# Conditioning matrix behind the first embedding summed on VectorE; first key slot computed one token tile at a time

## What is computed

```python
def per_layer_embed(h, p_i, g, w_gate, w_proj):
    gate = jax.nn.sigmoid((rms_norm(h, g) @ w_gate))
    return h + gate * (p_i @ w_proj)

# layer 1 of the first block
kvp = rms_norm(h, kv_norm) @ w_kv             # keys and values, 2048 columns
q = rms_norm(h, norm_mix[1]) @ b_w_q          # queries, 1024 columns
o = stick_breaking_attention(q, k, v)
h = h + o @ b_w_o

# second block
cond = jax.nn.silu(c)                         # 1 x 1024
mod = cond @ w_ada + b_ada                    # 1024 x 6144, 24 MB of weights
shift_m, scale_m, gate_m, shift_f, scale_f, gate_f = jnp.split(mod, 6, axis=-1)
h = modulate(rms_norm_2(x, g_pre_mix), shift_m, scale_m)
```

## Time and profile before

| | us |
|---|---|
| Median of 3 executions | 2948.27 |
| Lowest and highest of them | 2947.35, 2952.21 |
| The profiled execution | 2960.54 |
| Its span, first to last instruction | 2958.7 |
| PE busy | 2623.4 (89%) |
| DVE busy | 1368.7 (46%) |
| ACT busy | 616.2 (21%) |
| POOL busy | 489.4 (17%) |

### The profile page before, as it was taken

How to read it: one execution, slowest core, us unless ns; L and a number is a source line. 1 busy time by engine, 2 the same in 40 slices (tenths; PEclk the granted TensorE clock), 3 DMA queues, 4 the chain that set the end, 5 groups by cost and what they waited for, 6 DMA issues and landing times.

```text
span 2958.7 us, 28660 instructions
## 1 busy us (share of the span) xinstructions
PE 2623.4 (89%) x9706; PEld 1223.0 (41%) x9706; DVE 1368.7 (46%) x3391; ACT 616.2 (21%) x1232; POOL 489.4 (17%) x526
## 2 busy tenths in 40 slices
PE   8998787887799998787888799889999999999998
PEld 7663333333366663333333366543333232333333
DVE  5657777776425656777776541431111111111111
ACT  3022212232115122222232120211111111111111
POOL 0124333333200124333333200000000000000000
PEclk9999999999999999999999999889999999999999
DMA  5699999999863699999999833447999999899997
GB/s 217 264 377 422 421 421 421 421 420 421 347 240 143 249 377 422 421 421 421 421 421 421 345 127 114 180 199 321 422 422 422 422 422 422 352 422 422 376 400 295
DMA packets 145293, 1049.90 MB, mean 355 GB/s; under 512 B 16272, under 2 KB 16528, under 8 KB 17968
## 3 DMA queue, kind: packets, MB, share of 16 engines
q0 software_dynamic: 74064, 537.56, 43.8%
q1 hardware_dynamic: 70560, 509.12, 42.2%
q10 hardware_dynamic: 576, 2.13, 0.2%
HBM read 1047.69 MB, written 1.05 MB: 354 GB/s over the span
## 4 chain that ended last, share of the span: by engine, by line
PE 54%; DMA 37%; DVE 4%; ACT 2%; issue 1%; another core or an unknown queue 1%; DVEq 1%; SPq 0%; POOLq 0%
PE psum L566 14%; DMA big<-in_moe 13%; DMA uv_more<-in_peer_uv,rows_of 13%; DMA big<-in_peer_uv,rows_of 11%; PE psum L971 11%; PE psum L463 7%; PE psum L997 5%; PE psum L478 5%; PE psum L883 1%; PE psum L952 1%; PE psum L665 1%; PE psum L582 1%; DVE big L1598 1%; DVE uv_more L1598 1%; PE psum L965 1%
## 5 line engine op out<-in xcount | busy, mean ns | idle before, releaser
L566 PE MATMUL psum<-big,gdiag 128*128 128x512 f32 x1880 | 912.7, 642 | 233.1 <-ACT gdiag L1080 233.1
L1598 DVE CUSTOM_DVE_ANT_0 big<-psum,big 128x1024 f32<-128x1024 f32 x470 | 574.4, 1224 | 281.4 <-DMA big<-in_peer_uv,rows_of 274.8
L566 PEld LDWEIGHTS psum<-big,gdiag 128*128 128x128 f32 x1880 | 375.6, 205 | 761.9 <-issue 440.8
L2010 POOL DMA_INDIRECT big<-in_peer_uv,rows_of x470 | 444.7, 946 | 1158.2 <-PE psum L566 779.5
L971 PE MATMUL psum<-big 128*64 128x512 f32 x2240 | 500.9, 596 | 24.4 <-POOLq L2032 23.9
L1976 DVE TENSOR_SCALAR big<-psum 128x512 f32<-128x512 f32 x35 | 24.2, 692 | 667.5 <-PE psum L971 667.5
L971 PEld LDWEIGHTS psum<-big 128*64 128x64 f32 x2240 | 152.8, 137 | 370.7 <-issue 275.1
L997 PE MATMUL psum<-ring,big 128*64 128x512 f32 x1120 | 248.1, 594 | 3.8
L463 PE MATMUL psum<-big,ring 128*128 128x256 f32 x1088 | 241.2, 381 | 0.8 <-DVE big L1362 0.8
L463 PEld LDWEIGHTS psum<-big,ring 128*128 128x128 f32 x1088 | 206.5, 191 | 33.2 <-issue 3.8
L1074 ACT ACTIVATE gelu<-dots,rstd 128x4 f32<-128x4 f32 x128 | 38.0, 297 | 869.1 <-DVE dots L1598 869.1
(11 more groups left out here) (385 smaller groups left out, 1969.2 us busy)
## 6 DMA issues: line engine op xcount, KB each, us to landing
big<-in_moe SPq DMA_DIRECT2D x256, 1024.0 KB, 20.7
ring<-in_moe SPq DMA_DIRECT2D x128, 1024.0 KB, 19.4
big<-in_ada SPq DMA_DIRECT2D x24, 1024.0 KB, 11.8
ring<-in_peer_wq SPq DMA_DIRECT2D x16, 1024.0 KB
ring<-in_mix_in SPq DMA_DIRECT2D x14, 1024.0 KB
ring<-in_a_in SPq DMA_DIRECT2D x8, 1024.0 KB
ring<-in_ple_gate SPq DMA_DIRECT2D x8, 1024.0 KB
ring<-in_kv SPq DMA_DIRECT2D x8, 1024.0 KB
```

Source lines behind the costliest of these rows:

```text
L566: mm = pe.matmul(psum[:, OUT_BANK[t] + c, :], gdiag[:, n % DIAGS, :], uv[(PICKS * l + n) % ROWS][:, D + c * 512:D + (c + 1) * 512], start= ...
L1598: j = dve.tensor_tensor_reduce(out=u, in0=x, in1=u, scale=1.0, scalar=0.0, op0=ALU.mult, op1=ALU.add, accum_out=dots[:, n:n + 1])
L2010: pool.indirect_dma_start(uv[g % ROWS], None, table, bass.IndirectOffsetOnAxis(rows_of[:, n:n + 1], 0)).then_inc(uv_loaded[g % ROWS], 16)
```

## The change

Slots 4 to 7 of the conditioning are now summed on DVE by `sums`, as the others are: after `gains` of tile 1, four in a row. `condition_aside`, `take_aside` and `mod_rows` are gone; PE's four `turn_condition` stand after the second `qkv` slot. The turn of tile 0 (`turn(3, first, (0,), 6)`) stands between the two gate tiles, and DVE applies its two gains in `ple` (`first_gains`). The first `qkv` slot is done by `features_by_tile`, with the turn of tile 1 inside. `side` for part 1 lies elsewhere, since `qbT` and `xT2` now overlap its time.

```diff
             (4096, 6144, 2048, 8192, 10240, 12288, 14336, 16384),
-            (6144, 8192, 10240, 14336, 16384, 18432, 24576, 30720),
+            (8192, 10240, 14336, 16384, 18432, 22528, 24576, 30720),
...
             def turn_condition(s):
 
-                if 4 <= s < 8:
-                    pe.wait_ge(cond_took, s - 3)
-                    x = mod_rows[:, s % 2, :]
-                else:
-                    pe.wait_ge(sums_ready, s % 4 + s // 8 * 4 + 1)
-                    x = side[s // 4][s % 4 * 2][:, 0, :]
+                pe.wait_ge(sums_ready, s + 1)
+                x = side[s // 4][s % 4 * 2][:, 0, :]
...
                     mm.then_inc(tile_done, 1)
-                    if l and s == 0:
-                        turn(6, first, (0,), 6)
-                if l:
-                    return
-                pe.wait_ge(cond_ready, 1)
-                spare = ENDS[FIRST["ple_gate0"] + 1] % 3
-                condition_aside(4, 6)
-                condition_aside(5, 7)
-                turn_condition(4)
-                condition_aside(6, spare)
-                turn_condition(5)
-                pe.wait_ge(prod_taken, 2)
-
-            def last_condition():
-                turn_condition(6)
-                condition_aside(7, ENDS[FIRST["ple_gate0"] + 1] % 3)
-                turn_condition(7)
+                    if s == 0:
+                        turn(3 * l + 3, first, (0,), 6)
+
+            def features_by_tile(stage, i, known):
+
+                n = FIRST[stage]
+                w = slot_in(n).rearrange("p (k f) -> p k f", k=KC)
+                m = ENDS[n] - 2
+                for t in range(TT):
+                    if t:
+                        turn(i, hs, (1,))
+                    pe.wait_ge(xT_ready, known[t])
+                    for g in range(2):
+                        if t == 0:
+                            bank_free(m + g)
+                        for f in range(2):
+                            c = (2 * g + f) * P
+                            for k in range(KC):
+                                mm = pe.matmul(psum[:, (m + g) % 3, f * T + t * P:f * T + (t + 1) * P], w[:, k, c:c + P],
+                                               xT[:, k, t * P:(t + 1) * P], start=(k == 0), stop=(k == KC - 1))
+                        if t:
+                            mm.then_inc(tile_done, 1)
...
-            turn(3, first, (0,))
-            turn(3, hs, (1,))
-            last_condition()
-            pe.wait_ge(xT_ready, 20)
...
-            features("qkv", 0, xT)
+            features_by_tile("qkv", 3, (14, 20))
             features("qkv", 1, xT2)
+            for s in range(4, 8):
+                turn_condition(s)
+            pe.wait_ge(prod_taken, 2)
             pe.wait_ge(late_loaded, 16)
...
-                if l == 0:
-                    take_aside(4, 6)
-                    take_aside(5, 7)
                 root(7 + 7 * l, 1)
...
+            def first_gains(out, gain):
+
+                for b in range(2):
+                    dve.wait_ge(turned, 12 + b + 1)
+                    x = psum[:, 6 + b, :].rearrange("p (a b) -> p a b", a=4)
+                    k = slice(4 * b, 4 * b + 4)
+                    dve.tensor_tensor(out[:, k, 0:P], x, wide(gain[:, k], P), ALU.mult).then_inc(xT_ready, 1)
...
                 if l:
                     gains(6, gm, shift=shift_m, tiles=(0,), banks=6)
+                else:
+                    first_gains(xT, V8("kv_norm"))
                 dve.wait_ge(prod_done, 2 * l + 2)
...
                 j.then_inc(prod_taken, 1)
                 dve.drain()
+                if l == 0:
+                    first_gains(xT2, V8("norm_mix1"))
                 dve.tensor_tensor(h[:, 1, :], h[:, 1, :], ple_t[:, 1, :], ALU.add)
...
-            gains(3, V8("kv_norm"), gain2=V8("norm_mix1"))
+            gains(3, V8("kv_norm"), gain2=V8("norm_mix1"), tiles=(1,))
+            for s in range(4, 8):
+                sums(s)
             modulation(1)
```

More of the change, by code:

```diff
@@ L217, in build @@
             (4096, 6144, 2048, 8192, 10240, 12288, 14336, 16384),
[1 row of a table removed]
[1 row of a table added]
             (2048, 4096, 8192, 10240, 12288, 14336, 16384, 18432))]
         unit = sb("unit", [P, 1])
-        mod_rows = sb("mod_rows", [P, 2, 512])
         shift_m, scale_m, gate_m, shift_f, scale_f, gate_f = (modv[:, 8 * i:8 * i + 8] for i in range(6))
@@ L347, in build @@
         side_loaded = [sem(f"side_loaded{i}") for i in range(4)]
-        cond_took, aside_done = sem("cond_took"), sem("aside_done")
         rows_known, lru_exp, ro_taken = sem("rows_known"), sem("lru_exp"), sem("rec_out_taken")
@@ L506, in spread @@
                 mm.then_inc(row_done, 1)
[L508 to L517, removed]
-            def turn_condition(s):
-                if 4 <= s < 8:
-                    pe.wait_ge(cond_took, s - 3)
-                    x = mod_rows[:, s % 2, :]
-                else:
-                    pe.wait_ge(sums_ready, s % 4 + s // 8 * 4 + 1)
-                    x = side[s // 4][s % 4 * 2][:, 0, :]
+            def turn_condition(s):
+                pe.wait_ge(sums_ready, s + 1)
+                x = side[s // 4][s % 4 * 2][:, 0, :]
                 for j in range(4):
@@ L755, in _ @@
             pe.wait_ge(late_loaded, 32)
[L757 to L777, removed]
+            features_by_tile("mix_in", 6, (30, 32))
             pe.wait_ge(prod_taken, 4)
@@ L1127, in peer @@
                         exponents(p + 2)
[L1129 to L1133, removed]
             def ple(l):
@@ L1149, in ple @@
                     root(15, 1)
-                else:
-                    take_aside(6, ENDS[FIRST["ple_gate0"] + 1] % 3)
-                    take_aside(7, ENDS[FIRST["ple_gate0"] + 1] % 3)
             peer(0, 1)
```

## The result

| | before | changed |
|---|---|---|
| Median, us | 2947.81 (8 executions) | 2957.72 (8 executions) |
| Lowest and highest, us | 2940.69, 2954.46 | 2951.57, 2960.48 |
| Ratio, 95% interval | | 1.0032 [1.002, 1.0044] |
| Gates end to third `qkv` slot, us | 41.3 | 47.5 (predicted 48.5) |
| PEER's last add to first scores, us | 64.6 | 73.5 |

The change makes the kernel slower, by 0.32%, about 9.4 us (5.9 to 13.0 by the interval). The forecast was 2956.4, with 0.74 on slower.

What follows compares the result with a forecast made beforehand. PE was taken as the bound, then the first key slot's landing at 848.5 us, then DVE's sums. The third slot starts at 887.8 instead of 879.7, so 2948.3 + 8.1 = 2956.4 us, range 2950.5 to 2960.5.

Steps and rivals of the forecast that it cites:

- Gates end: End of PE's two gate tiles, with tile 0's turn between them: 839.3 instead of 838.4 us, 0.9 us later.
- Key slot in use: First key slot's weights, queued behind the conditioning halves, land at 848.5 us (847.4 to 849.5); PE idles 9.2 us.
- `first_gains` and the later scaling of tile 1: On DVE: gains for `xT2` cost 1.2 us, tile 1 scaled near 846.2; no cost, since PE waits for weights.
- First pass at the low clock: First key slot for tile 0 on PE, after the idle time: 10.05 us instead of 7.38 at full clock.
- Turn to gains, and gains: Tile 1 between the passes: gains start 0.69 us after the turn's first transpose and take 2.47, ending at 861.7.
- DVE the bound at the fourth partition sum: Before the third slot, PE is ready at 885.9 and waits for DVE's sums until 886.8, 0.9 us.
- Third slot: Start of the third `qkv` slot on PE: 887.8 instead of 879.7 us, 8.1 us later.
- Behind it the lists are alike: After the third slot's start both kernels have the same lists, so the 8.1 us stay unchanged.
- Carried to the end: The 8.1 us at the third slot reach the kernel's end in full: 2948.3 + 8.1 = 2956.4 us.
- The second pass slow: Rival, first key slot's tile 1 pass also at low clock: +9.9 us, 2958.2; chance 0.25.
- Weights in time: Rival, key slot lands without delaying PE after the gates: 3.8 us sooner than before, 2944.5; chance 0.08.
- The shift swallowed: Rival, a later wait on a transfer issued at a fixed place absorbs the shift: 2948.3 +- 2; chance 0.07.

Runs made afterwards that it cites:

- e5: Changed kernel with 10 filler matmuls, result unread, in PE's idle time between the second gate tile and the first pass; ratio to before 1.0028.
- e6: Kernel before with only the load order edited: first key slot issued behind four of eight conditioning halves; ratio to before 1.0012.
- e7: Kernel before with only the first key slot divided by token tile, the turn of tile 1 inside it; ratio to before 1.0009.
- e3: Changed kernel with 20 filler matmuls, result unread, on PE between the second gate tile and the first pass; ratio to before 1.006.
- e1: Changed kernel with the first key slot's load issued behind four of eight conditioning halves instead of behind all eight; ratio to before 1.0008.
- e9: Changed kernel with the key slot issued behind four conditioning halves and the four partition sums spread between quarter slots; 2940.52 against 2947.26 before, ratio 0.9981.
- e2: Changed kernel with the first key slot undivided, behind the turn and gains of tile 1; ratio to before 1.002.
- e4: Changed kernel with the four partition sums together behind the third slot's second quarter instead of ahead of that slot; ratio to before 1.0045.
- e8: Changed kernel with the four partition sums one at a time between quarters of the third and fourth slots; ratio to before 1.0023.
- e10: Changed kernel with key slot issued behind four conditioning halves and partition sums spread, but first key slot undivided; ratio to before 1.0015.

## Why the prediction was right

Times of the changed kernel are put on before's by adding 6.25 us, the difference of the two A.

- **Gates end**, predicted 839.3: 833.01 + 6.25 = 839.3. The turn between the gate tiles cost its 0.9 us.
- **Key slot in use**, 848.5 (847.4 to 849.5): 848.3. The trace of the changed kernel shows the landings that the one before did not: 839.44 and 842.0, that is 845.7 and 848.3, and PE starts with the second. They are 2.57 us apart, where I had taken 2.54 for each MB.
- **`first_gains` and the later scaling of tile 1**, at nothing: PE waited for weights at that time in any case, and DVE scaled tile 1 at 839.06 + 6.25 = 845.3, ahead of them.
- **First pass at the low clock**, 10.05: 9.68, from 842.01 to 851.69, at 0.50 at its start. e5 shows that the fall alone is worth 2.5 us.
- **Turn to gains, and gains**, 0.69 and 2.47: 0.64 and 2.40. **Sums**, 25.0: 24.8.
- **DVE the bound at the fourth partition sum**, by 0.9: 0.92 idle, released by L1406.
- **Third slot**, 887.8, +8.1: 886.8, +7.1. The small terms (landing, pass, gains, sums) were each a few tenths too long.
- **The step that was missing** is behind it: "Behind it the lists are alike" is true of the lists and not of the clock. The third slot's first quarter took 5.39 us, not the 3.6 to 3.7 of a full clock, since the granted clock fell behind 16 one-column matmuls in a row. I had priced the four sums at 0.98 each and nothing more. That makes +8.9 at the first scores. A further fall at 953 makes +10.6 at the projection; e6 and e7 have a fall at the suffix matmuls too, so it need not come from the change.
- **Carried to the end**: +10.6 in L or +8.9 without that last fall, +9.4 by the ratio (5.9 to 13.0). The median stands 1.3 us from the forecast within a range of 10. That it is so near is in part luck: the sum was 1.0 us too high at the third slot and left out 1.8 us right behind it.

*The second pass slow* did not happen in the changed kernel: 7.41 us, behind the turn and 2.14 us of idle. It happened in e3 with the same turn and the same idle time. The Trainium skill, "TensorE: Matmul & The Clock Gate", section "Part 4: PE-mode transpose", says that transposes don't count as busy for the clock gate in the same way; the turn stands in both, so the rule alone doesn't decide it.

*Weights in time* did not happen either; the key slot landed behind the conditioning halves, at the step of the others. e1 and e9 then brought the case about on purpose. My estimate for it, 3.8 us sooner than before, rested on DVE's 25 us and a full clock; e1 gave 3.0 later, e9, in which the attention no longer waits for DVE's sums, 5.5 sooner.

*The shift swallowed* is excluded: the ratio's interval lies above 1, and over the runs of the table the ratio follows L.

## What to carry to other kernels

Work taken from an engine also covered something. Ask which transfer was hidden behind it, move that load in its queue together with the work, and judge the two edits as one: here the same load order costs 0.12% without the change and wins back three quarters of the loss with it. A division that lets one tile start early is worth something only when what it waits for, here the weights, is there by then. Compare two profiles by a stretch between events that both have, not by their spans, and look in it for falls of the clock in parts that no edit touches: here each moved it by 1.7 us.

## What was not expected of the hardware

Small matmuls in a row were followed by a lower granted clock, in e2 and e4 with PE busy all the time: 16 of one column, 3.6 us in all, were followed by 0.50 in five kernels of six that had them together (in three of these with 0.9 us of idle ahead of the last four), and a quarter slot then took 5.4 to 6.2 us in place of 3.7. Four of them between larger matmuls (e8, e9, e10) were not.

A short idle time is followed by a lower clock on some occasions and not on others. In the changed kernel the clock fell here, in stretches of PE alone, while nearly the same idle time (1.97 us) left it at 1.00 in the earlier trace rows:

```profile
952.54 0.49 PE L698 MATMUL psum<-big 128*128 128x128 f32 x2 [2.02 <-DVEq L1637]
```

```profile
952.00:954.00 2.00, 1.46 (x4) 0.75 0.00 0
954.00:956.00 2.00, 2.00 (x7) 0.50 0.00 0
```

The 2.14 us around the turn did the same in e3 and not in the changed kernel, e1, e4, e5, e7, e8 and e9. What makes the difference stays open; no run was made for it. Also open is how much of e1's 10.2 us, for 5 us of bytes, is the cost of a queue that was nearly dry when the load was issued: that was seen, and its effect was not tested by itself.
